# Two transformer-like blocks on one core: three norms through two columns, and eight low halves on another engine

## What is computed

```python
# first block
x = x + conv_mixers(rms_norm(x, norm_mix_g), w_in, ..., w_mix_out)
x = x + memory_cross_attention(rms_norm(x, norm_xa_g), rms_norm(mem, norm_mem_g), w_q, w_kv, w_xo)
x = x + peer_ffn(rms_norm(x, norm_peer_g), w_peer_q, subkeys, u, v)   # 8 heads x 16 experts per token
x = rms_norm(x, final_norm_g)
# second block
h = rmsnorm(x, pre_norm_mix)
...                                              # two attentions, gated and merged
x = x + rmsnorm(merged @ w_out, post_norm_mix)
h2 = rmsnorm(x, pre_norm_mlp)
y = square(relu(h2 @ w_up)) @ w_down
x = x + rmsnorm(y, post_norm_mlp)
# where
def rmsnorm(x, g):
    return x * rsqrt(mean(x * x, axis=-1) + EPS) * g
```

## Time and profile before

| | us |
|---|---|
| median of 3 runs (lowest to highest) | 1491.51 (1491.06 to 1495.69) |
| the profiled execution | 1493.7 |
| its span in the trace | 1491.9 |
| TensorE busy | 1312.2 (88%) |
| VectorE busy | 979.4 (66%) |
| ScalarE busy | 519.7 (35%) |
| GpSimd busy | 561.5 (38%) |
| low halves on GpSimd, 49 of them | 228.7 |
| low halves on VectorE, 53 of them | 127.8 |

### The profile page before, as it was taken

One profiled execution on the slowest core, in us unless ns is written; L12 is line 12 of the kernel. 1 busy time (PEld: TensorE's weight loads), 2 busy tenths in 40 slices (PEclk: granted clock), 3 DMA queues, 4 the chain that ended last, 5 costly groups with the idle time before them and its releaser, 6 DMA issues.

```text
span 1491.9 us, 25940 instructions
## 1 busy us (share of the span) xinstructions
PE 1312.2 (88%) x10024; PEld 1253.7 (84%) x10024; DVE 979.4 (66%) x2091; ACT 519.7 (35%) x990; POOL 561.5 (38%) x348
## 2 busy tenths in 40 slices
PE   6999999999888797796968886878899999889996
PEld 5999999988888797796968786878785889889996
DVE  4679986766688585859585768755424447683574
ACT  4633456445442121211112221211226455434341
POOL 1588843221455455354535364545002000022220
PEclk9999999999999989898999899999999999999999
DMA  6555544452389999999999999999830135245450
GB/s 238 213 192 175 188 168 168 158 196 87 112 327 420 421 422 422 422 422 422 422 420 420 421 420 422 422 422 422 359 142 0 57 114 174 100 156 201 162 195 32
DMA packets 58088, 397.39 MB, mean 266 GB/s; under 512 B 6289, under 2 KB 9873, under 8 KB 10385
## 3 DMA queue, kind: packets, MB, share of 16 engines
q0 software_dynamic: 36864, 268.45, 43.3%
q1 hardware_dynamic: 21136, 127.76, 24.2%
HBM read 395.14 MB, written 1.05 MB: 266 GB/s over the span
## 4 chain that ended last, share of the span: by engine, by line
PE 52%; DMA 21%; DVE 13%; issue 8%; ACT 3%; POOL 2%; DVEq 0%; POOLq 0%; ACTq 0%; SPq 0%
DMA rows_late<-peer_uv_dram,stage 21%; PE bank L703 11%; PE bank L705 11%; PE bank L704 11%; PE bank L677 6%; PE bank L914 6%; DVE rows_late L1870 4%; ACT w_hi L1110 2%; PE bank L689 1%; POOL rows_late L620 1%; PE bank L808 1%; DVE hid L2054 1%; POOL w_lo L516 1%; DVE rstd L1442 1%; PE bank L832 1%
## 5 line engine op out<-in xcount | busy, mean ns | idle before, releaser
L516 POOL TENSOR_TENSOR w_lo<-raw,w_hi 128x2048 fp32r<-128x2048 f32 x49 | 228.7, 4669 | 489.8 <-ACT w_hi L1110 489.8
L914 PE MATMUL bank<-h_norm,rows_late 128*128 128x128 f32 x2816 | 328.8, 279 | 30.3 <-ACT h_norm L1274 30.3
L914 PEld LDWEIGHTS bank<-h_norm,rows_late 128*128 128x128 f32 x2816 | 324.9, 196 | 33.4 <-ACT h_norm L1274 33.4
L1870 DVE SCALAR_TENSOR_TENSOR rows_late<-rows_late,squares 128x1024 f32<-128x1024 f32 x176 | 213.8, 1229 | 134.2 <-DMA rows_late<-peer_uv_dram,stage 125.1
L914 PE MATMUL bank<-h_norm,rows_early 128*128 128x128 f32 x1280 | 176.4, 305 | 94.7 <-ACT h_norm L1274 94.7
L914 PEld LDWEIGHTS bank<-h_norm,rows_early 128*128 128x128 f32 x1280 | 170.3, 219 | 101.2 <-ACT h_norm L1274 101.1
L620 POOL DMA_INDIRECT rows_late<-peer_uv_dram,stage x165 | 196.8, 1193 | 131.7 <-PE bank L914 77.7
L1110 ACT ACTIVATE w_hi<-raw 128x2048 fp32r<-128x2048 f32 x102 | 194.3, 1906 | 59.7 <-PE bank L705 49.7
L703 PE MATMUL bank<-x_hi_b,w_hi 128*128 128x256 f32 x640 | 186.9, 292 | 13.8 <-DVE x_lo_b L1474 4.9
L703 PE MATMUL bank<-x_hi_a,w_hi 128*128 128x256 f32 x672 | 191.6, 285 | 4.7 <-DVE x_lo_a L1472 2.3
L704 PE MATMUL bank<-x_lo_a,w_hi 128*128 128x256 f32 x672 | 190.8, 284 | 0.0
(11 more groups left out here) (303 smaller groups left out, 2016.9 us busy)
## 6 DMA issues: line engine op xcount, KB each, us to landing
raw<-w_in_dram SPq DMA_DIRECT2D x28, 1024.0 KB, 5.0
raw<-w_up_dram SPq DMA_DIRECT2D x16, 1024.0 KB, 4.9
raw<-w_down_dram SPq DMA_DIRECT2D x16, 1024.0 KB, 4.9
rows_late<-w_in_dram SPq DMA_DIRECT2D x10, 1024.0 KB, 13.6
raw<-w_kv_dram SPq DMA_DIRECT2D x8, 1024.0 KB, 4.9
raw<-w_peer_q_dram SPq DMA_DIRECT2D x8, 1024.0 KB, 5.0
raw<-sc_w_out_dram SPq DMA_DIRECT2D x4, 1024.0 KB, 4.9
raw<-cf_w_pw_dram SPq DMA_DIRECT2D x4, 1024.0 KB, 4.9
```

The source lines that it names most:

```text
L516: api.tensor_tensor(ring(w_lo, i), ring(raw, i), ring(w_hi, i).bitcast(F32), ALU.subtract).then_inc(w_lo_ready[LO_BY[i][0]], 1)
L914: mm = nc.tensor.matmul(ct(Y_ACC[c][t // 4], t % 4, P), expert_rows(k)[:, D + t * P:D + (t + 1) * P], ct(diag, k % DIAGS, P), start=False, ...
L1870: w_.scalar_tensor_tensor(out=row, in0=row, scalar=1.0, in1=h_tok[:, c * D:(c + 1) * D], op0=ALU.mult, op1=ALU.mult, accum_out=pre[:, side ...
```

## The change

Part one: the range `BY_DVE` of loads whose low halves VectorE makes starts at the first load of the k layer rather than at load 62. Part two: for the norms peer, post_mix and post_mlp the mean is made with one column per chunk of 128 tokens, the tile of squares now being the weights, so that each token is a partition. Root and reciprocal are of 128x2. TensorE then spreads each column over all partitions: the column, repeated 128 times, is the weights and the identity the moving matrix. The products read the result from PSUM (`RSTD_PS`). VectorE waits for the two spreads inside `rstd_of`; TensorE waits for the reciprocal in `spread`, right behind `stat_sum`.

```diff
-BY_DVE = range(LOAD_OF["pq", 12], LOAD_OF["up", 6])
+BY_DVE = range(LOAD_OF["k", 0], LOAD_OF["up", 6])
...
+BY_TOKEN = ("peer", "post_mix", "post_mlp")
...
+        RSTD_HALVES = [psum[7][:, SEQ + c * P:SEQ + (c + 1) * P] for c in range(NC)]
...
-                    mm = nc.tensor.matmul(STAT[:, 0:SEQ], mean_d[:], ct(squares, k), start=(k == 0), stop=(k == tiles[-1]))
+                    if name in BY_TOKEN:
+                        for c in range(NC):
+                            mm = nc.tensor.matmul(STAT[:, c:c + 1], ct(squares, k)[:, c * P:(c + 1) * P], mean_d[:, 0:1],
+                                                  start=(k == c == 0), stop=(k == tiles[-1] and c == NC - 1))
+                    else:
+                        mm = nc.tensor.matmul(STAT[:, 0:SEQ], mean_d[:], ct(squares, k), start=(k == 0), stop=(k == tiles[-1]))
                 mm.then_inc(stat_ready, 1)
+
+            def spread(name):
+
+                pe.wait_ge(inverted, BY_TOKEN.index(name) + 1)
+                for c in range(NC):
+                    nc.tensor.matmul(RSTD_HALVES[c], rstd_col[:, c:c + 1].to_broadcast([P, P]), ident,
+                                     start=True, stop=True).then_inc(rstd_spread, 1)
...
             stat_sum("peer")
+            spread("peer")
...
-                s.activation(root_buf[:], STAT[:, 0:SEQ], ACT.Sqrt, bias=eps[:, 0:1]).then_inc(rooted, 1)
+                out, n = (root_col, NC) if name in BY_TOKEN else (root_buf, SEQ)
+                s.activation(out[:], STAT[:, 0:n], ACT.Sqrt, bias=eps[:, 0:1]).then_inc(rooted, 1)
...
                 dve.wait_ge(rooted, ROOTS.index(name) + 1)
-                link(w_.reciprocal(rstd[:] if to is None else to, root_buf[:]))
+                if name in BY_TOKEN:
+                    w_.reciprocal(rstd_col[:], root_col[:]).then_inc(inverted, 1)
+                    dve.wait_ge(rstd_spread, NC * (BY_TOKEN.index(name) + 1))
+                    return RSTD_PS
+                to = rstd[:] if to is None else to
+                link(w_.reciprocal(to, root_buf[:]))
+                return to
```

More of the change, by code:

```diff
@@ L279, in two_blocks @@
         root_buf = sb("root_buf", SEQ)
+        root_col = sb("root_col", NC)
+        rstd_col = sb("rstd_col", NC)
         eps = sb("eps", 1)
@@ L480, in two_blocks @@
         inverse_ready = sem("inverse_ready")
+        inverted = sem("inverted")
+        rstd_spread = sem("rstd_spread")
         counts = {}
@@ L1051, in _ @@
             stat_sum("post_mix")
+            spread("post_mix")
             for half in range(2):
@@ L1062, in _ @@
             stat_sum("post_mlp")
+            spread("post_mlp")
             assert tile[0] == len(TILES)
@@ L1482, in norm_split @@
             def norm_split(name, src, gain, dst, x):
-                rstd_of(name)
+                by = rstd_of(name)
                 k = NORMS[NORM_AT[name]][1]
@@ L1488, in norm_split @@
                         done(w_.scalar_tensor_tensor(out=ct(dst, i), in0=ct(src, i), scalar=v(gain, i),
-                                                     in1=rstd[:], op0=ALU.mult, op1=ALU.mult), normed)
+                                                     in1=by, op0=ALU.mult, op1=ALU.mult), normed)
                     if i:
```

## The result

The changed kernel takes 1477.95 us (median of 4, 1476.69 to 1479.23). The kernel before took 1493.18 us (median of 4) in the same session. The ratio is 0.9897, 95% interval 0.9876 to 0.9919: 15.2 us or 1.0% less.

The account below looks back on a forecast made before the run. TensorE carries half the chain, gather DMA a fifth, VectorE 13%; the gain was sought where TensorE waits. Halves -3.8 and norms -2.55 make -6.35 us, from 1491.51 to 1485.2 us, range 1481.5 to 1489.5.

Parts of the forecast that it names:

- one stream of fixed bytes that starts sooner: Gather stretch behind peer: gathers move fixed bytes and only start earlier, so time gained ahead is kept; no term of its own.
- Rival 3: More comes back: no clock fall behind peer 1.5 us, larger norms 0.9, better sc 1.2; typical -9, 1482.5 us; chance 0.15.
- The moved low halves: Eight low halves go from GpSimd to VectorE, between 195 and 391 us: -3.8 us in sum.
- Load 38, sc: Sc layer: TensorE's pause shrinks from 2.4 to about 1.25 us and the clock doesn't fall: 2.65 us back.
- the softmax stretch: Stretch where TensorE paused up to 1.3 us and the clock stayed at 1.00; cited for no clock fall in sc.
- rival 1: Clock still falls at the sc stop (+1.45), mix is near its upper bound (+1.5): -3.4, 1488.1 us; chance 0.16.
- Load 47, mix: Mix layer: VectorE waits for ScalarE's high half with additions queued behind: +0.7 us, from -0.5 to +2.2.
- Load 56, xo: Xo layer: the peer norm's root starts sooner, TensorE's 1.9 us stop nearly goes: -1.6 us, from -1.0 to -2.1.
- the list of six: Six places where VectorE instructions stand still while GpSimd works: 21.5 us returned, against 18.3 us for eight halves.
- The three norms: Peer, post_mix, post_mlp: root to first product 1.45 us instead of 2.30, 0.85 saved in each: -2.55 us.
- Rival 2: Norms: the way VectorE to TensorE and back costs what shorter root and reciprocal save: -3.8, 1487.7 us; chance 0.12.
- Rival 4: VectorE becomes the bound from 195 to 376 us, every moved half on the path: +9.5, 1501.0 us; chance 0.07.

Follow-up runs that it names:

- P: Kernel before plus 16 unused words, so weight buffers and expert rows sit 64 B on, at a multiple of 256 B: 1482.69 us, ratio 0.994 to before.
- e10: Changed kernel, VectorE's low halves after each second tile in pw, mix, xo, xa reciprocal before load 50's half, two sc gates sooner: 1477.31 us, 0.9888 to before.
- e20: Changed kernel with small tensors moved and 48 unused words: rows and weights at a multiple of 256 B, x_a, x_b, hid 192 B off weights: 1458.94 us.
- e16: Placement of e20, with the later low halves of e10 and the third sc tile's half taken sooner: 1460.99 us, ratio 0.9782 to the kernel before.
- N: The three norms by columns; alone, with buffers at the old place, against the kernel before: 1490.37 us, ratio 0.9986.
- H: The eight low halves moved to VectorE; alone, with buffers at the old place, against the kernel before: 1492.84 us, ratio 0.9997.

## Why the prediction was wrong, and where it was right

*The step that failed* is in the paragraph on what bounds the kernel: "The change touches neither gathers nor matrix products, so its worth lies where TensorE waits for another engine." The trace carried the sentence as far as instructions go. It overlooked that the diff adds two tensors in the middle of a list that is placed in order. The fifth of the chain that is DMA was left out of the sum as "one stream of fixed bytes that starts sooner"; the bytes were fixed and their rate was not. The missing term is P, -11.0 us by four pairs of kernels, 9.9 of them in the gather stretch, and none of the rivals had it. Rival 3, more comes back, had the right sign and the wrong reason: its 9 us were to come from the clock behind peer, larger norms and a better sc.

*The moved low halves*, -3.8 us: right as a walk up to the first gather, 3.55 us on average, and too large for the whole time, -1.4 (by its uncertainty between 0.2 more and 3.0 less). The step that failed stands in the norms' paragraph and was taken over for the halves: that the gathers are "one stream of fixed bytes that starts sooner", and so what is gained ahead of them is gained at the end. By place:
- Load 38, sc: the stop is 0.9 us, not 1.25, and behind it the clock stayed at 1.00, as the softmax stretch had suggested. All 2.65 us came (2.75 by the spacing of the matmuls), and rival 1's condition for sc did not.
- Load 47, mix: VectorE waits 1.96 us for ScalarE in front of three of the layer's four halves, with the additions behind it, and the q layer gets its new stop of 1.10 us. This is the walk as it was told. e10 shows that another order takes those stops away.
- Load 56, xo: TensorE's 1.9 us before the peer statistic are gone.
- No VectorE instruction is above 2.3 us in the stretches named, as forecast; one half of 2.5 us stands between them, at 254.0. The low halves moved onto VectorE don't stall.
- VectorE's total fell by 10.3 us, 4.7 of them from the shorter reciprocals. The halves give the other 5.6, where 18.3 - 21.5 is 3.2; the list of six left out the low half at 219.29, which took 3.58 us beside GpSimd.

*The three norms*, -2.55 us: right, -2.8 in the whole time, with an uncertainty of 1.6. The term is 1.03 us in each of the three instead of 0.85. The root took 0.26 where 0.20 was put down and the reciprocal 0.17, as forecast; the spread was mis-sized: reciprocal's end to first product is 0.80 us, and the prediction had taken 1.0 from a pair of wider matmuls. The estimate that was set beside it from the Trainium skill ("TensorE: Matmul & The Clock Gate", section "Single matmul latency") was 0.6 us and left out the way to VectorE; the page gives its formula for a bf16 matmul, and these are fp32. The measured 0.80 lies half way between the two. Rival 2, the spread gives nothing, is excluded by the three traces.

*Rival 4*, VectorE becomes the bound: no run came near it. In e20 and e16, where TensorE is quicker, low halves on GpSimd and VectorE stop it more, a mild form of it.

*The chances.* 0.63 for faster was given with a forecast of 0.4%. Without P the same change measures 0.9981 (0.9971 to 0.9991), within 0.3%; over both places N and H make 0.28%, at the edge of it. That the time came out clearly lower is luck as far as this reasoning goes: three quarters of the gain are P, a term that it didn't have.

## What to carry to other kernels

- Read a diff for what it allocates, not only for what it executes. Where tensors are placed one behind the other, two columns of 8 B move every buffer behind them; write down the addresses before and after, modulo 256 B, of all that a DMA fills and of both operands of the matmuls. Place such buffers on purpose, and keep the placement fixed when an instruction-level edit is to be judged (an unused tensor of the right size does it).
- When a change moves the time by more than its own parts can, look for the part of the span that nobody touched. Here one line of the page, the rate in the gather slices, gave it away; with three suspects, all eight combinations cost eight kernels and give each part four times over.
- A gain ahead of a long DMA-bound stretch shows in its first instruction, and here only in part in the total. Quote both.

## What the hardware showed that was not expected

- DMA into SBUF: 427 GB/s where the 8 KB rows begin at a multiple of 256 B, 421 to 422 where they begin at 64, 128 or 192 past one. With the five early sets alone in place 423 to 425, with the eleven late ones 426 to 428.
- Matmuls of 256 columns in a stream, rounded (fp32r) weights and moving tensor both from SBUF: 0.1200 us each at distance 0 modulo 256 B, in all of twelve kernels; 0.1133 or 0.1178 at 192, the best of those tried; 0.1133 to 0.1200 in between. Two paces occur at one distance and one clock, so the distance is not all. With 192 for the x_a, x_b and hid products it is worth 17 us here by the ratios (e20 against the changed kernel), more than anything that the change itself did.
- The way from VectorE through two small TensorE matmuls and back to VectorE, with a column that is spread over 128 partitions, takes 0.80 us, with TensorE idle for 0.6 us before it; in post_mix and post_mlp the granted clock around it is 1.00.
